# A Fourier stage with its odd frequencies from tokens split by parity, and its gating on GpSimd

## The reference, cut to what matters

```
ug = u.reshape(b, length, 4, 256)                      # length 2048
spec = fft over tokens and over the channels of a group, real part, ortho
y = spec @ w_four[group] + b_four
y_f = y * silu(gate_f)
```

## Time and profile before

| what | value |
|---|---|
| median of 3 runs | 2140.97 us (2137.82 to 2141.24) |
| profiled execution | 2139.17 us, its span 2137.4 us |
| busy, share of the span | TensorE 97%, weight loads 83%, VectorE 72%, ScalarE 25%, GpSimd 3% |
| Fourier stage, groups 0 to 3 | about 1625 to 1757 us of the span |
| output stage, first a part | from 1790.57 us |

### The profile page before, as it was taken

One profiled execution on the slowest core, in us unless ns is written; L12 is line 12 of the kernel. 1 busy time (PEld: TensorE's weight loads), 2 busy tenths in 40 slices (PEclk: granted clock), 3 DMA queues, 4 the chain that ended last, 5 costly groups with the idle time before them and its releaser, 6 DMA issues.

```text
span 2137.4 us, 51183 instructions
## 1 busy us (share of the span) xinstructions
PE 2069.1 (97%) x21168; PEld 1769.7 (83%) x21168; DVE 1530.5 (72%) x3274; ACT 538.1 (25%) x966; POOL 74.8 (3%) x109
## 2 busy tenths in 40 slices
PE   5899999999999999999999999999997999999997
PEld 2799988898888888888888888888887887888886
DVE  4865854144878878788878788799998885565554
ACT  3621134211122212212122222122214343222221
POOL 0001101000000000000000000000000010000000
PEclk9999999999999999999999999999999999999999
DMA  9534555322424333343334243334335476445351
GB/s 376 192 124 146 173 167 148 115 82 91 139 85 138 109 104 118 107 126 106 119 97 135 90 125 116 102 122 125 110 98 199 188 261 222 153 136 180 132 182 59
DMA packets 227006, 299.08 MB, mean 140 GB/s; under 512 B 15011, under 2 KB 155967, under 8 KB 223452
## 3 DMA queue, kind: packets, MB, share of 16 engines
q1 hardware_dynamic: 142332, 178.38, 25.6%
q10 hardware_dynamic: 74096, 81.18, 11.4%
q0 software_dynamic: 10352, 36.25, 5.3%
HBM read 198.16 MB, written 97.59 MB: 138 GB/s over the span
## 4 chain that ended last, share of the span: by engine, by line
PE 88%; DVE 6%; DMA 2%; ACT 1%; issue 1%; SPq 1%; ACTq 0%; DVEq 0%
PE all_bank L61 20%; PE all_bank L63 19%; PE all_bank L62 19%; PE all_bank L1487 5%; PE all_bank L1493 5%; PE all_bank L1490 5%; PE all_bank L1565 3%; PE all_bank L1341 2%; PE all_bank L1521 2%; PE all_bank L1508 2%; PE all_bank L1558 1%; PE all_bank L71 1%; PE all_bank L1547 1%; PE all_bank L1340 1%; DMA front_w_mod<-in_w_ada 1%
## 5 line engine op out<-in xcount | busy, mean ns | idle before, releaser
L61 PE MATMUL all_bank<-hidden_h_hi,head_hi 128*128 128x512 f32 x718 | 288.1, 401 | 0.0
L63 PE MATMUL all_bank<-hidden_h_hi,head_lo 128*128 128x512 f32 x718 | 280.3, 390 | 0.0
L62 PE MATMUL all_bank<-hidden_h_lo,head_hi 128*128 128x512 f32 x718 | 279.9, 390 | 0.0
L1603 ACT ACTIVATE head_projected<-all_bank 128x512 f32<-128x512 f32 x148 | 88.6, 599 | 728.3 <-PE all_bank L63 460.9
L1487 PE MATMUL all_bank<-hidden_h_hi,head_hi 128*128 128x512 f32 x466 | 191.9, 412 | 0.7 <-DVE head_lo L1645 0.2
L1701 DVE RECIPROCAL head_inverse<-head_gate 128x448 f32<-128x448 f32 x64 | 185.2, 2931 | 0.0
L1493 PE MATMUL all_bank<-hidden_h_hi,head_lo 128*128 128x512 f32 x466 | 182.2, 391 | 0.0
L1490 PE MATMUL all_bank<-hidden_h_lo,head_hi 128*128 128x512 f32 x466 | 181.8, 390 | 0.0
L63 PEld LDWEIGHTS all_bank<-hidden_h_hi,head_lo 128*128 128x128 f32 x718 | 134.8, 188 | 28.7
L61 PEld LDWEIGHTS all_bank<-hidden_h_hi,head_hi 128*128 128x128 f32 x718 | 134.9, 188 | 27.6
L62 PEld LDWEIGHTS all_bank<-hidden_h_lo,head_hi 128*128 128x128 f32 x718 | 135.0, 188 | 25.5
(11 more groups left out here) (323 smaller groups left out, 4780.2 us busy)
## 6 DMA issues: line engine op xcount, KB each, us to landing
head_raw<-in_w_in POOLq DMA_DIRECT2D x37, 512.0 KB, 4.9
head_value<-value_rows SPq DMA_DIRECT2D x64, 256.0 KB, 4.7
head_query<-piece_query SPq DMA_DIRECT2D x64, 256.0 KB, 5.6
head_out<-head_o ACTq DMA_DIRECT2D x64, 256.0 KB, 2.6
tail_o<-head_out SPq DMA_DIRECT2D x32, 512.0 KB, 5.8
front_raw<-in_w_in SPq DMA_DIRECT2D x19, 512.0 KB, 4.9
front_stage<-in_x SPq DMA_DIRECT2D x16, 512.0 KB, 7.8
front_w_mod<-in_w_ada SPq DMA_DIRECT2D x8, 1024.0 KB, 13.8
```

What stands on the lines that cost most here:

```text
L61: nc.tensor.matmul(out, st_hi, mv_hi, start=start, stop=False)
L62: nc.tensor.matmul(out, st_hi, mv_lo, start=False, stop=False)
L63: return nc.tensor.matmul(out, st_lo, mv_hi, start=False, stop=stop)
L1603: nc.scalar.activation(projected[unit % 2][:], ps_proj[unit % 2][:], PIECES[name][1], scale=PIECES[name][2]).then_inc(proj_copied, 1)
```

## The change

1. The odd frequencies get a third fold as well, by parity of the token: in `front` and `tail`, `by_parity`, `in_order` and `of_time` order the tokens of the arrays 1 and 3 as 256 even ones, then 256 odd ones. Even tokens give the same value at frequency k and at its mirror, odd tokens the opposite one, so only 256 columns of each are computed: `waves` has 24 products of 256 columns for a = 1 and 3 too, and all four tables have half of their rows.
2. `combine(odd)` puts the halves together again: two steps of 512 into a new tile `mixed`, then four of 256 into `y`, with the bias. The even combination adds the bias too; `copy_top` as well.
3. The gating of turns 0 to 5 moves to GpSimd, four products of 512 each, without bias. The last two turns stay on VectorE as `gate_last_y`. There are two `y` tiles; a combination waits for the gating two turns before.
4. TensorE's waits before a = 1 and 3 go by the new `odd_mixed`. The middle rows in `front` are ordered by parity, in two steps each in place of one.

GpSimd's queue is now: gatings 0 to 4, wait for the last low split of `fold`, two loads of weights, gating 5, wait for the last middle product, two loads, and on as before.

```diff
+        def gate_y(m):
+            n, c = m // 2, m % 2
+            pool.wait_ge(g_here[c], (n + 1) * DMA)
+            pool.wait_ge(combined, 2 * m + 2)
+            pool.wait_ge(top_copied, m + 1)
+            for a in range(4):
+                last = pool.tensor_tensor(array(g[c], a), array(y[c], a), array(g[c], a), ALU.mult)
+            last.then_inc(y_gated, 1)
+
+        for m in range(2 * FG - 3):
+            gate_y(m)
         pool.wait_ge(fold_lo_done, 4 * FG)
         load_w(KT)
         load_w(KT + 1)
+        gate_y(2 * FG - 3)
         pool.wait_ge(mid_done, FG)
...
             if odd:
-                nc.vector.tensor_tensor(y[:, 1:HALF:2], cos[:], sin, ALU.subtract)
-                nc.vector.tensor_tensor(y[:, SEQ - 1:HALF:-2], cos[:], sin, ALU.add).then_inc(combined, 1)
+                wait_count(v, combined, 2 * m)
+                nc.vector.tensor_tensor(mixed[:, 0, :], cos[:], sin, ALU.subtract)
+                nc.vector.tensor_tensor(mixed[:, 1, :], cos[:], sin, ALU.add).then_inc(odd_mixed, 1)
+                v.wait_ge(odd_mixed, m + 1)
+                (less_0, less_1), (more_0, more_1) = ([mixed[:, i, j * EIGHTH:(j + 1) * EIGHTH] for j in range(2)] for i in range(2))
+                nc.vector.scalar_tensor_tensor(out[:, 1:QUART:2], less_0, bias, less_1, ALU.add, ALU.add)
+                nc.vector.scalar_tensor_tensor(out[:, HALF + 1:HALF + QUART:2], less_0, bias, less_1, ALU.add, ALU.subtract)
+                nc.vector.scalar_tensor_tensor(out[:, SEQ - 1:SEQ - QUART:-2], more_0, bias, more_1, ALU.add, ALU.add)
+                nc.vector.scalar_tensor_tensor(out[:, HALF - 1:HALF - QUART:-2], more_0, bias, more_1, ALU.add, ALU.subtract).then_inc(combined, 1)
...
-        def gate_y(n, c):
-            m = 2 * n + c
+        def gate_last_y(c):
+            m = 2 * FG - 2 + c
             v.wait_ge(combined, 2 * m + 2)
             v.wait_ge(top_copied, m + 1)
-            v.wait_ge(g_here[c], (n + 1) * DMA)
-            nc.vector.scalar_tensor_tensor(g[c][:], y[:], b_cols[:, m:m + 1], g[c][:], ALU.add, ALU.mult).then_inc(y_gated, 1)
+            v.wait_ge(g_here[c], FG * DMA)
+            wait_count(v, y_gated, m)
+            nc.vector.tensor_tensor(g[c][:], y[c][:], g[c][:], ALU.mult).then_inc(y_gated, 1)
...
-                if m:
-                    pe.wait_ge(combined, 2 * m - 1 if a in (0, 2) else 2 * m)
-                if a % 2:
-                    for t in range(QT):
-                        done = mm3(nc, ps_y[a][:], p_hi[a][:, t, ch], p_lo[a][:, t, ch], tab_hi[a][:, t, :], tab_lo[a][:, t, :],
-                                   t == 0, t == QT - 1)
+                if m and a % 2:
+                    pe.wait_ge(odd_mixed, m)
+                elif m:
+                    pe.wait_ge(combined, 2 * m - 1)
```

More of the change, by code:

```diff
@@ L307, in front, with by_parity @@
     PAIRS = 2 * KT
+    def by_parity(dst, src):
+        return ((dst[:, 0:GRP].rearrange("p (two m) -> p two m", two=2), src[:, 0:GRP].rearrange("p (m two) -> p two m", two=2)),
+                (dst[:, GRP:HALF], src[:, GRP:HALF]))
     def step_of(s):
@@ L556, in mid_rows_low @@
         def mid_rows_low():
-            v.wait_ge(mid_high_done, 2)
-            nc.vector.tensor_tensor(mid_st[2 * MID_AT:2 * MID_AT + FG, :], mid_rows[:, 0:HALF], mid_st[0:FG, :].bitcast(F32),
-                                    ALU.subtract).then_inc(mid_ready, 1)
+            v.wait_ge(mid_high_done, 4)
+            low, high = (by_parity(mid_st[at:at + FG, :], mid_rows) for at in (2 * MID_AT, 0))
+            for (dst, src), (rounded, _) in zip(low, high):
+                nc.vector.tensor_tensor(dst, src, rounded.bitcast(F32), ALU.subtract).then_inc(mid_ready, 1)
         def tokens_low(s):
@@ L753, in mid_rows_high @@
             for i in range(2):
[L754 removed]
+                for dst, src in by_parity(mid_st[i * MID_AT:i * MID_AT + FG, :], mid_rows):
+                    nc.scalar.activation(dst, src, ACT.Copy).then_inc(mid_high_done, 1)
         def evacuate_middle(j):
@@ L2001, in array, with in_order, of_time @@
         return ap[:, a * QUART:(a + 1) * QUART]
+    def in_order(ap, a):
+        return ap.rearrange("p (two m) -> p two m", two=2) if a % 2 else ap
+    def of_time(ap, a):
+        return ap.rearrange("p (m two) -> p two m", two=2) if a % 2 else ap
     def a_set(t):
@@ L2063, in load_w, with pieces_stored @@
             sp.dma_start(w[:], w_fourier[n * FC:(n + 1) * FC, :].rearrange("(c p) d -> p c d", p=P)).then_inc(w_four_here, DMA)
+        def pieces_stored(n):
+            heads_done = 2 * n + 2
+            for sem in left.proj_stored:
+                sp.wait_ge(sem, min(left.units_of_head * heads_done, left.all_units) // 2 * DMA)
         def load_g(n, c):
@@ L2382, in _ @@
             combine(n, 0, 1)
-            gate_y(n, 0)
+            if last:
+                gate_last_y(0)
             if not last:
@@ L2396, in _ @@
             combine(n, 1, 1)
-            gate_y(n, 1)
+            if last:
+                gate_last_y(1)
         v.wait_ge(hn_here, DMA)
@@ L2474, in copy_sine @@
             act.wait_ge(y_done, y_turn(m, 2 + odd))
-            wait_count(act, combined, 2 * m)
+            if odd:
+                wait_count(act, odd_mixed, m)
+            else:
+                wait_count(act, combined, max(2 * m - 1, 0))
             nc.scalar.activation(sine[:, odd, :], ps_y[2 + odd][:], ACT.Copy).then_inc(sine_copied, 1)
```

71 lines of the change are left out of this document (36 added, 35 removed).

## The result

The changed kernel takes 2144.4 us (median of 10 runs, 2143.0 to 2148.8) against 2138.8 us of the kernel before beside it: ratio 1.0026, interval 1.0017 to 1.0035. It is slower by 5.6 us. (Three kernels of the study, and once the kernel before, had one execution that took 2968 to 4080 us at a low clock; the ratios leave these out.) The forecast was no change, 2140 us; the slow rival (2147) named the right side.

What follows compares the result with a forecast made beforehand. TensorE was taken to bound groups 1 and 2. Group 0 +0.2, groups 1 and 2 -3.6, group 3 +2.9 gave -0.5, kept at the output stage; clock +0.5 made 0: 2140.0 us, range 2131 to 2149.

Steps and rivals of the forecast that it cites:

- the slow rival: GpSimd also loses to splits of `p`, second-turn gatings 6.9 us, clock's 2 us added: 2147 us, 2145 to 2151; chance 0.20.
- The bound of before: Fourier stage, groups 1 and 2: TensorE sets the pace at 30.5 us a group, VectorE works about 25.0.
- the price of the odd products: Odd products go from 0.228 to 0.119 us apart, saving TensorE 5.2 us a group, 20.9 us in eight turns.
- The lock: GpSimd's first-turn gating and VectorE's four low splits of `fold` exclude each other; VectorE loses 3.4 us a group.
- nothing is won: Group 0, bound by VectorE before and after: +0.2 us to the end of its second turn's odd combination.
- The ring: Gating, store and issues, channel weights landing, their products, odd combination: 29.9 us in group 1, 27.5 in group 2, together -3.6.
- the clock term: TensorE's products slowed to 1.2 GHz after idle stretches of some 5 us: 0.5 us, bounds 0 and 6.
- Group 3: Last group of the Fourier stage, up to the first use of the Fourier rows: +2.9 us.
- The late second pair: Group 3: second pair of output weights waits behind the sixth gating; its split starts 15.4 us behind the combination: +5.0.
- given back: Group 3: VectorE's present waits for the next pair of output weights and small gaps vanish, 3.8 us.
- its first cause: Splits of `p` also hold up GpSimd, so second-turn gatings take 6.9 us; decided once the second gating is over 6.2.
- The start of the output stage: Behind the Fourier rows: last gating +1.0, 1 to 2 us come back from loads; start moves -0.5, between -1.5 and +1.5.

Runs made afterwards that it cites:

- `gpsimd_only`: Against the kernel before: first six gatings on GpSimd, two y tiles, bias in the combinations; odd products stay at 512 columns. 2144.3 us, ratio 1.0019.
- `warm`: Changed kernel plus 64 and 22 products nobody reads, ahead of TensorE's wait for the channel weights of groups 2 and 3; ratio 1.0002 to the kernel before.
- `pool_ahead`: Changed kernel with the second pair of output weights issued before the sixth gating in GpSimd's queue instead of behind it; 2142.8 us, ratio 1.0018 to the kernel before.
- `vector_gate`: Changed kernel with the gating of all eight turns back on VectorE, the parity split kept; 2139.1 us, ratio 1.0003 to the kernel before.
- `weights_first`: Changed kernel with the low split of the first channel weights moved ahead of the low splits of `fold`; single execution, only its rows used, no time given.

## Why the prediction was wrong, point by point

**The bound of before** (TensorE, 5.5 us of VectorE in reserve) and the price of the odd products were right. The odd combination was put at 2.85 us and took 3.0.

**The lock** was put on VectorE, 3.4 us a group. `gpsimd_only` shows this very size (5.79 against 2.49 us), so the reading of the earlier trace rows was right for a kernel with the old combination. In the changed kernel its own new steps shut GpSimd out. So group 0, where "nothing is won" was forecast (+0.2 up to the end of the second turn's odd combination), came out at -3.6: from M0 it is 28.6 us (1636.41 to 1664.98) for 32.1. The check that I had named, "if the low splits of `fold` keep 0.69 us the time is under 2136", failed as well: VectorE was no longer near the path that set the end.

**The ring** was seen: its links and their order are those of the chain above. Its size was not. From the end of one group's last odd combination to the next it is 35.4 us for group 1 (1664.98 to 1700.38) and 30.7 for group 2 (to 1731.08) instead of 29.9 and 27.5. Link by link for group 1: gating 5.1 for 4.6; store and issues 1670.24 to 1677.82, 7.6 for 5.0; landing 6.7 for 7.0; weights' products 5.6 for 2.95; the rest, to the end of the odd combination, 10.3 for 10.05. For group 2: gating +0.5, store and issues 4.2 as forecast, landing -0.3, products +2.6, the rest +0.3. Groups 1 and 2 came out at +5.1 instead of -3.6 us.

**The failed step is the clock term.** I put it at 0.5 us with bounds 0 and 6, arguing that the products behind the first idle stretch are short. They are, but they lie on the ring, and there were two such stretches: my own ring of group 2, 27.5 us, was already 2.2 us longer than TensorE's work of 25.3, and I counted no idle stretch for it. In the profiled execution it cost twice 2.6 us, 5.3 of the 8.7 by which groups 1 and 2 missed. `warm` agrees: 5.2 us of time, give or take 3. The size isn't the same in every execution. `pool_ahead` has the same ring and nearly the same waits, and the 24 products of the weights take 4.5 and 4.4 us there, some 3 us dearer in all; the timeline of TensorE:

```profile
1684.51 3.60 PE L2683 MATMUL all_bank<-tail_w,tail_chan 128*128 128x128 f32 x16 [7.58 <-DMA tail_w<-in_w_fourier]
...
1713.79 2.62 PE L2683 MATMUL all_bank<-tail_w,tail_chan 128*128 128x128 f32 x16 [2.63 <-DMA tail_w<-in_w_fourier]
```

The changed kernel's profiled execution is on the dear side: its mean granted clock is 0.983, that of its nine others 0.984 to 0.986. So the term is 3 to 5 us where I had 0.5. The next largest part is the first store with the issues behind it, 7.6 us for 5.0: this store takes 5.79 us, the one in group 2 only 3.83. A gate load issued at 1668.30, 1.9 us ahead of it, may share the queues with it; that this is the cause is not tested.

**Group 3** was +4.4 us (to the first Fourier row split, from the last odd combination of group 2) instead of +2.9. The late second pair was right in kind and size: the split starts 14.9 us behind the combination, forecast 15.4. Too much was counted as given back: TensorE idles 6.83 us there, and products 0.21 us apart follow that too. `pool_ahead` takes 4.9 us out of this group in its profile, but only 1.7 us of the time, which is within the noise.

**The rivals.** The slow rival had the right sign and nearly the right number (2147) by luck, since its first cause was wrong: it wanted the second gating to be over 6.2 us. It was 5.1, so splits of `p` hold GpSimd up by hardly anything (eight splits beside it, one input in PSUM; 1.29 to 1.31 us a step, and 1.26 to 1.27 where VectorE idles). What it named as a mere addition, the clock's 2 us, was the main part. By my own sum with the clock at 5.3 instead of 0.5 the change would have cost 4.8 us; measured 5.6. The other errors (group 0 -3.8, the other links of the ring +3.4, group 3 +1.5, what follows it -0.7) add up to +0.4. That they nearly cancel is luck: the gain of group 0, which I had denied, hides the slower links of the ring.

**The start of the output stage** was forecast to keep its distance from the first split of Fourier rows. The first a part came 0.9 us later (35.2 us behind that split, before 34.3). The second came 0.7 us earlier, which the sum had not: the half-clock stretch of the earlier trace rows behind the first a part is gone, where TensorE idled 1.23 instead of 1.94 us, and the two a parts stand 15.9 us apart instead of 17.5.

## What to carry to other kernels

An idle stretch of TensorE is to be priced with what runs behind it: if products on the critical chain follow, they can cost up to twice their time, and it can pay to fill a wait with products that nobody reads or, better, to move the wait. When a step is moved to a slower engine, follow every queue behind it to its last reader; here two loads that depended on nothing of it (the channel weights, and the head outputs) stood behind a store only by program order, and putting the first of them ahead gave 11 us, twice what the change had cost. Saved work on a bound engine can be worth nothing until the ring around it is opened: the halved products gave nothing measurable with the ring closed and some 5 us with it open.

## What the runs showed of the hardware

**The clock.** Behind idle stretches of 8.01, 2.98 and 2.92 us TensorE's products took twice their time (granted clock 0.51 in 1668 to 1674 of `vector_gate`), and behind the 1.94 us of the earlier trace rows too; behind 1.23 us in the changed kernel the clock stayed at 1.00. In between both happened: behind 1.59 us in `vector_gate` (1648.64) it fell to 0.50 in 1650.0 to 1653.3, behind 1.90 us in `gpsimd_only` (1738.40) it stayed at 1.00 up to 1745. So the length of the stretch before alone does not tell. Products of 256 columns stood 0.213 us apart at the lower level and 0.12 at the upper. The Trainium skill (TensorE: Matmul & The Clock Gate, "Wait — 56ns, not 53.3ns?") has columns divided by 1.2 GHz at the lower level, by my estimate from it 213 ns for 256, which the trace matches; for the upper it gives columns by 2.4 GHz and 2.5 ns, estimated 109 ns for 256, where the rows show 0.12 us.

**The lock.** That a two-input step of VectorE and one of GpSimd exclude each other shows in both directions where both inputs lie in SBUF (splits of 1.78 us for 0.68 in `gpsimd_only`, a GpSimd step of 3.42 for 1.29 in the changed kernel). New is who gets the turn between back-to-back steps: an unbroken row of VectorE's two-input steps kept GpSimd out for 2.1 us in each of the three first-turn gatings of the changed kernel, and in `weights_first` one step that reads PSUM ahead of the same row made them alternate. The Trainium skill (SBUF — State Buffer, "SBUF: two separate sides") says that whichever starts first has the ports for the whole instruction; the trace agrees for single steps, but this does not say that a row of VectorE's steps is not interrupted. At the sixth gating of the changed kernel the splits are of 1024 elements:

```profile
1731.33 2.34 DVE L2291 TENSOR_TENSOR tail_w_lo<-tail_w_raw,tail_w_hi 128x1024 fp32r<-128x1024 f32 x2
```

They keep their pace, and GpSimd's first step took 3.60 us although the profile has it start 0.1 us ahead of them and a step reading PSUM stood before. What decides there stays open.

**GpSimd.** A step of 512 elements with two SBUF inputs takes 1.26 to 1.27 us where VectorE idles (changed kernel, 1683.66 to 1687.37) and 1.29 to 1.31 beside splits of `p`, not the 1.13 that I had worked out from the earlier trace rows by subtraction.
